# The last pair of experts: prompt sums first, sample rows by halves, one tile scaled by GpSimd

## What is computed

```python
hid = silu(einsum('becd,edf->becf', xs, w_gate)) * einsum('becd,edf->becf', xs, w_up)
out = einsum('becf,efd->becd', hid, w_down) * gate_vals[..., None]
moe = zeros_like(h).at[bidx, idx].add(out)
x = x + g2 * moe
y = rmsnorm(x, norm_final)          # y_prompt (128 rows), y_sample (512 rows)
```

## Time and profile before

| | us |
|---|---|
| median of three runs | 1007.59 |
| the three runs | 1007.21, 1007.59, 1008.83 |
| the profiled execution, its own time | 1008.96 |
| its span in the profile | 1007.2 |
| TensorE busy in the span | 965.1 (96%) |
| VectorE, ScalarE, GpSimd busy | 357.0, 294.7, 101.3 |
| mean granted TensorE clock | 0.990 of full speed |

### The profile page before, as it was taken

How to read it: one execution, slowest core, us unless ns; L and a number is a source line. 1 busy time by engine, 2 the same in 40 slices (tenths; PEclk the granted TensorE clock), 3 DMA queues, 4 the chain that set the end, 5 groups by cost and what they waited for, 6 DMA issues and landing times.

```text
span 1007.2 us, 18254 instructions
## 1 busy us (share of the span) xinstructions
PE 965.1 (96%) x7982; PEld 430.9 (43%) x7982; DVE 357.0 (35%) x806; ACT 294.7 (29%) x482; POOL 101.3 (10%) x112
## 2 busy tenths in 40 slices
PE   4999899999999899998999999999999999999996
PEld 3554456666666554463232332322323223232232
DVE  2476666463653563664021020210212102112115
ACT  5237756573653654323010010100101001010012
POOL 3200010000000011212001102011010110200100
PEclk9999999999999999999899999999999999999998
DMA  9990004504028441233999999999999999999982
GB/s 349 356 346 0 1 25 155 173 6 168 6 90 312 200 150 63 84 126 138 389 427 397 413 424 408 418 399 412 422 394 417 400 414 406 396 414 405 409 348 104
DMA packets 45218, 276.06 MB, mean 274 GB/s; under 512 B 3920, under 2 KB 4080, under 8 KB 32880
## 3 DMA queue, kind: packets, MB, share of 16 engines
q1 hardware_dynamic: 37824, 253.24, 62.2%
q0 software_dynamic: 5824, 16.81, 5.6%
q10 hardware_dynamic: 1520, 5.28, 1.4%
HBM read 262.30 MB, written 13.01 MB: 273 GB/s over the span
## 4 chain that ended last, share of the span: by engine, by line
PE 79%; DVE 7%; DMA 5%; ACT 3%; issue 3%; SPq 2%; POOL 1%; POOLq 0%; DVEq 0%
PE pa L538 52%; PE p L538 24%; DMA ring<-in_w_ada_dram 3%; DMA ring<-in_w_up_dram 1%; SPq L389 1%; ACT reg_c L1149 1%; PE pa L1043 1%; DMA reg_c<-h_rows,row_p 1%; ACT L1149 1%; PE p L981 1%; ACT reg_b L1149 1%; DVE reg_c L1550 1%; DVE reg_c L1595 1%; POOL reg_d L476 0%; ACT reg_d L1149 0%
## 5 line engine op out<-in xcount | busy, mean ns | idle before, releaser
L538 PE MATMUL pa<-ring,reg_b 128*32 128x512 f32 (+1 forms) x3232 | 412.8, 595 | 1.3 <-ACT reg_b L1149 1.2
L538 PEld LDWEIGHTS pa<-ring,reg_b 128*32 128x32 f32 (+1 forms) x3232 | 128.8, 114 | 256.3 <-issue 255.8
L538 PE MATMUL pa<-reg_a,ring 128*128 128x512 f32 (+1 forms) x768 | 229.6, 454 | 2.6 <-ACT reg_d L1149 2.6
L538 PE MATMUL p<-ring,reg_b 128*16 128x512 f32 x1536 | 172.9, 594 | 0.2 <-DMA ring<-in_w_up_dram 0.2
L538 PEld LDWEIGHTS pa<-reg_a,ring 128*128 128x128 f32 x768 | 119.3, 192 | 96.5 <-issue 96.4
L1149 ACT ACTIVATE reg_b<-pa 128x512 f32<-128x512 f32 (+1 forms) x36 | 21.1, 608 | 426.8 <-PE pa L538 262.1
L538 PEld LDWEIGHTS p<-ring,reg_b 128*16 128x16 f32 x1536 | 45.0, 97 | 121.3 <-issue 120.7
L1889 DVE TENSOR_TENSOR reg_b<-reg_b,p 128x512 f32<-128x512 f32 x8 | 5.5, 687 | 235.0 <-PE p L538 235.0
L1149 ACT ACT_TABLE_LOAD x64 | 82.1, 1283 | 4.2 <-issue 2.9
L1913 DVE SCALAR_TENSOR_TENSOR reg_c<-pa,slot_s,reg_c 128x512 f32<-128x512 f32 x14 | 10.5, 750 | 101.6 <-PE pa L538 101.6
L1149 ACT ACTIVATE reg_c<-reg_c 128x320 f32<-128x320 f32 (+1 forms) x86 | 43.3, 574 | 10.1 <-DVE reg_c L1601 9.2
(11 more groups left out here) (307 smaller groups left out, 742.9 us busy)
## 6 DMA issues: line engine op xcount, KB each, us to landing
ring<-in_w_gate_dram SPq DMA_DIRECT2D x32, 2048.0 KB, 14.5
ring<-in_w_up_dram SPq DMA_DIRECT2D x32, 2048.0 KB, 16.0
ring<-in_w_down_dram SPq DMA_DIRECT2D x32, 2048.0 KB, 17.7
ring<-in_w_ada_dram SPq DMA_DIRECT2D x12, 2048.0 KB, 8.0
ring<-in_w_in_dram SPq DMA_DIRECT2D x7, 2048.0 KB, 21.2
ring<-in_w_out_dram SPq DMA_DIRECT2D x2, 2048.0 KB, 19.2
sum_rows<-reg_a ACTq DMA_DIRECT2D x5, 512.0 KB, 2.7
h_rows<-reg_d POOLq DMA_DIRECT2D x5, 512.0 KB, 3.0
```

The lines of the kernel that those rows point to most:

```text
L538: return nc.tensor.matmul(out, lhsT, rhs, start=start, stop=stop, **kw)
```

## The change

In the last pair TensorE ends the prompt's down sums before the sample's second half begins, both halves of the prompt's in one go. It then does half of the first 512 columns of the sample's second sums, the prompt tile's two `add_rows`, the other half, and the last 512 columns. After that come all eight sample products in the order of `LAST_ROWS`: tiles 0 and 1 with their left halves, then with their right halves, then tiles 2 and 3. The PSUM tiles are given out anew in `last_in`. VectorE and ScalarE follow the new order: the prompt's tile is added, squared and scaled first, and the scalings of tiles 1, 2 and 3 come behind all additions. Tile 0 is no longer scaled by VectorE. GpSimd multiplies it by `nf_row` into `first_scaled` (the region `reg_b`), waits for the reciprocal from VectorE, multiplies again by that, and stores the tile from its own queue. SyncE stores the four other tiles, in the order 4, 1, 2, 3.

```diff
--- before.py
+++ after.py
@@ -213,6 +213,10 @@
         count_row = reg_e[:, 512:512 + T]
         g2q = reg_e[:, 0:512]
         which = reg_d[:, 2 * D:2 * D + T]
+
+        LAST_ROWS = [(4, 0), (4, 1), (0, 0), (1, 0), (0, 1), (1, 1), (2, 0), (2, 1), (3, 0), (3, 1)]
+        last_in = (p67, pa[0], p45, pa[1], pa[0])
+        first_scaled = reg_b[:, 0:D]
         out_q = reg_d[:, 2 * D + T:2 * D + T + 512]
         row_f = sp[:, 0:2, 0]
 
@@ -400,11 +404,11 @@
                     sp_eng.wait_ge(added[e][kind], 16 * (PAIRS - 1))
             for i in range(NT):
                 sp_eng.dma_start(acc[:, i, :], sum_rows[i * P:(i + 1) * P, :]).then_inc(back, 16)
-            for i in range(NT):
-                sp_eng.wait_ge(f_y, i + 1)
+            for n, i in enumerate((NT - 1, 1, 2, 3)):
+                sp_eng.wait_ge(f_y, n + 1)
                 dst = y_sample[0, i * P:(i + 1) * P, :] if i < NT - 1 else y_prompt[0]
                 sp_eng.dma_start(dst, acc[:, i, :]).then_inc(y_dma, 16)
-            sp_eng.wait_ge(y_dma, NT * 16)
+            sp_eng.wait_ge(y_dma, (NT - 1) * 16)
 
 
         @block.gpsimd
@@ -529,7 +533,15 @@
                 pool.sem_inc(out_free, 1)
             pool.wait_ge(g_s, 16 * PAIRS)
             pool.wait_ge(g_p, 16 * PAIRS)
-            pool.wait_ge(st_dma, 16 * (1 + 2 * HEADS))
+            pool.wait_ge(nf_in, 16)
+            pool.wait_ge(fin_add, LAST_ROWS.index((0, 1)) + 1)
+            nc.gpsimd.tensor_tensor(first_scaled, acc[:, 0, :], nf_row, ALU.mult).then_inc(pool_step, 1)
+            pool.wait_ge(pool_step, 4 + NT)
+            pool.wait_ge(h_ready, NT + 1)
+            nc.gpsimd.tensor_tensor(first_scaled, first_scaled, stat[:, 3, 0:1].to_broadcast([P, D]), ALU.mult).then_inc(pool_step, 1)
+            pool.wait_ge(pool_step, 5 + NT)
+            pool.dma_start(y_sample[0, 0:P, :], first_scaled).then_inc(st_dma, 16)
+            pool.wait_ge(st_dma, 16 * (2 + 2 * HEADS))
 
 
         @block.tensor
@@ -986,20 +998,19 @@
                     r = nc.tensor.transpose(dst[:, k * 32:(k + 1) * 32], xg_p[:, k * P:(k + 1) * P], ident[0:32, 0:32])
                 r.then_inc(xp_ps, 1)
 
-            def add_rows(i):
-
-                dst = (pa[0], p67, pa[1], p45, pa[0])[i]
-                if i == NT - 1:
-                    pe.wait_ge(fin_add, 2)
-                for half in range(2):
-                    cols = slice(512 * half, 512 * half + 512)
-                    pe.wait_ge(out_done, 3 * PAIRS + (1 + half if i < 3 else 3))
-                    if i < NT - 1:
-                        r = mm(dst[:, cols], which[:, i * P:(i + 1) * P], out_s[:, cols])
-                    else:
-                        rows = slice(64 * half, 64 * half + 64)
-                        r = mm(dst[:, cols], which[rows, TS:T], out_q[rows, :])
-                    r.then_inc(oh_ps, 1)
+            def add_rows(i, half):
+
+                cols = slice(512 * half, 512 * half + 512)
+                if i < NT - 1:
+                    pe.wait_ge(out_done, 3 * PAIRS + 2 + half)
+                    if i == 1:
+                        pe.wait_ge(fin_add, 2)
+                    r = mm(last_in[i][:, cols], which[:, i * P:(i + 1) * P], out_s[:, cols])
+                else:
+                    rows = slice(64 * half, 64 * half + 64)
+                    pe.wait_ge(out_done, 3 * PAIRS + 1)
+                    r = mm(last_in[i][:, cols], which[rows, TS:T], out_q[rows, :])
+                r.then_inc(oh_ps, 1)
 
             def pair(i, head, last=False):
                 def use(m, kh):
@@ -1114,16 +1125,17 @@
                     prompt_sums("d", 1, hidden_p, p45[:, 512:1024])
                 else:
 
+                    prompt_sums("d", 0, hidden_p, p45[:, 512:1024])
                     use("d", 1)
-                    sample_sums("d", 1, 0, hsT, pa[1]).then_inc(d_ps, 1)
+                    prompt_sums("d", 1, hidden_p, p45[:, 512:1024])
+                    sample_sums("d", 1, 0, hsT, pa[1], (0, 1))
+                    pe.wait_ge(which_done, 1)
+                    for t, half in LAST_ROWS[0:2]:
+                        add_rows(t, half)
+                    sample_sums("d", 1, 0, hsT, pa[1], (2, 3)).then_inc(d_ps, 1)
                     sample_sums("d", 1, 1, hsT, pa[1]).then_inc(d_ps, 1)
-                    prompt_sums("d", 0, hidden_p, p45[:, 512:1024])
-                    pe.wait_ge(which_done, 1)
-                    for t in range(3):
-                        add_rows(t)
-                    prompt_sums("d", 1, hidden_p, p45[:, 512:1024])
-                    for t in range(3, NT):
-                        add_rows(t)
+                    for t, half in LAST_ROWS[2:]:
+                        add_rows(t, half)
 
             pe.wait_ge(at_done, NT - 1)
             turn_rows(0)
@@ -1422,12 +1434,12 @@
                 rows_in(i + 1)
             hidden(PAIRS - 1)
             chain(A(stat[:, 2, 0:1], eps[:, 0:1], ACT.Sqrt))
-            for i in range(NT):
-                act.wait_ge(fin_add, 2 * i + 2)
-                if i >= 2:
-                    act.wait_ge(f_ss, i - 1)
-                A(h_tok[i % 2], acc[:, i, :], ACT.Square, accum_out=stat[:, 0, i:i + 1]).then_inc(f_ss, 1)
-                act.wait_ge(f_ss, i + 1)
+            for n, i in enumerate((NT - 1, 0, 1, 2, 3)):
+                act.wait_ge(fin_add, LAST_ROWS.index((i, 1)) + 1)
+                if n >= 2:
+                    act.wait_ge(f_ss, n - 1)
+                A(h_tok[n % 2], acc[:, i, :], ACT.Square, accum_out=stat[:, 0, i:i + 1]).then_inc(f_ss, 1)
+                act.wait_ge(f_ss, n + 1)
                 A(stat[:, 2, i:i + 1], stat[:, 0, i:i + 1], ACT.Sqrt, bias=eps[:, 0:1], scale=1.0 / D).then_inc(f_std, 1)
 
 
@@ -1948,41 +1960,37 @@
                 cols_ = slice(half * 512, half * 512 + 512)
                 V.tensor_tensor(out_s[:, cols_], pa[1][:, cols_], g2r[0][:, cols_], ALU.mult).then_inc(out_done, 1)
 
-            sample_out(0)
-            sample_out(1)
-
-            def add_rows(i):
-                src = (pa[0], p67, pa[1], p45, pa[0])[i]
-                if i == 0:
-                    dve.wait_ge(back, 16 * NT)
-                for half in range(2):
-                    cols_ = slice(512 * half, 512 * half + 512)
-                    dve.wait_ge(oh_ps, 2 * i + half + 1)
-                    V.tensor_tensor(acc[:, i, cols_], acc[:, i, cols_], src[:, cols_], ALU.add).then_inc(fin_add, 1)
-
-            def final_scale(i):
-                dve.wait_ge(f_std, i + 1)
+            def add_rows(i, half):
+                n = LAST_ROWS.index((i, half))
+                cols_ = slice(512 * half, 512 * half + 512)
+                dve.wait_ge(oh_ps, n + 1)
+                V.tensor_tensor(acc[:, i, cols_], acc[:, i, cols_], last_in[i][:, cols_], ALU.add).then_inc(fin_add, 1)
+
+            def final_scale(n, i):
+                dve.wait_ge(f_std, n + 1)
                 chain(V.reciprocal(stat[:, 3, i:i + 1], stat[:, 2, i:i + 1]))
                 V.scalar_tensor_tensor(acc[:, i, :], acc[:, i, :], stat[:, 3, i:i + 1], nf_row, ALU.mult,
                                        ALU.mult).then_inc(f_y, 1)
 
-            def prompt_out():
-                s, turn = chunk("d", 1, 1)
-                dve.wait_ge(freed[s], last * 2 + turn + 1)
-                V.tensor_tensor(out_q, p45[:, 512:1024], g2q, ALU.mult).then_inc(out_done, 1)
-
+            s, turn = chunk("d", 1, 1)
+            dve.wait_ge(freed[s], last * 2 + turn + 1)
+            V.tensor_tensor(out_q, p45[:, 512:1024], g2q, ALU.mult).then_inc(out_done, 1)
             dve.wait_ge(nf_in, 16)
-            add_rows(0)
-            add_rows(1)
-            final_scale(0)
-            add_rows(2)
-            final_scale(1)
-            prompt_out()
-            final_scale(2)
-            add_rows(3)
-            add_rows(4)
-            final_scale(3)
-            final_scale(4)
+            dve.wait_ge(back, 16 * NT)
+            add_rows(4, 0)
+            add_rows(4, 1)
+            sample_out(0)
+            final_scale(0, 4)
+            sample_out(1)
+            for i, half in LAST_ROWS[2:8]:
+                add_rows(i, half)
+
+            dve.wait_ge(f_std, 2)
+            V.reciprocal(stat[:, 3, 0:1], stat[:, 2, 0:1]).then_inc(h_ready, 1)
+            for i, half in LAST_ROWS[8:]:
+                add_rows(i, half)
+            for n, i in ((2, 1), (3, 2), (4, 3)):
+                final_scale(n, i)
 
 
 _INS = ["x_prompt", "x_sample", "state_lru", "state_hgrn", "c", "c_ctx", "w_ada", "b_ada", "norm_mix", "w_in",
```

## The result

The changed kernel is slower: 1011.46 us median of ten runs, against 1008.72 us for ten runs of the kernel before. The ratio is 1.0033 (95% interval 1.0025 to 1.0041); it is estimated from all the runs, and the quotient of the two medians alone is 1.0027. The forecast was 1008.2 us in a range of 1006.7 to 1009.5, and no difference that can be told, so it missed. Three single executions of the later measurements, two of the kernel before and one of the kernel with the last tile by halves, took 27% longer or more and are in no ratio.

The account below looks back on a forecast made before the run. TensorE was taken to carry the chain almost to the end, followed by VectorE's scalings and the stores. TensorE -1.01, scalings +0.56 and queued stores +1.10 gave +0.65 us on 1007.59, so 1008.2 us, range 1006.7 to 1009.5.

Parts of the forecast that it names:

- the sum: At the kernel's end: TensorE -1.01, three scalings in a row +0.56, queued stores +1.10, together +0.65 us.
- GpSimd's final wait for its store ends near 1004.5: End of GpSimd's queue: the wait for tile 0's store ends before SyncE's, with no cost in the sum.
- Without this cover: Earlier wait for `back`: loads land by about 978, addition needs them at 986.1, no cost; uncovered, the rest of that landing.
- the filled stall: TensorE's stall from 995.48 to 996.56, 1.08 us, is filled, so TensorE ends 1.01 us earlier, at 998.30.
- Three scalings at a pitch of 1.40 us: VectorE behind the last addition: scalings end at 1000.59, 1001.99 and 1003.39, where the last ended at 1003.84 before.
- The four stores: Last stores share the DMA engines, 5.20 us from 1001.42 to 1006.62, 0.65 us later than before; bounds 0.45 and 0.8.
- the product by the spread column: GpSimd's second product for tile 0, by the reciprocal: 997.73 to 1000.11, with its store issued at 1000.41.
- Exclusion between VectorE and GpSimd: First last scaling against GpSimd's second product: nothing or 0.9 us, equally open, said to hardly matter.
- The rival by which it costs 0.9 us: Stores free, VectorE held by GpSimd's product: last scaling ends at 1004.3, 0.45 us later than before, 1008.0 us; chance 0.14.
- a late second product: GpSimd's second product waits for all VectorE's scalings, its store ends 2.6 us later than before: 1010.2 us; chance 0.06.

Follow-up runs that it names:

- the last tile by halves: Against the kernel in which ScalarE, not GpSimd, makes tile 0's second scaling and stores it: tile 3 scaled and stored in two 512-column halves; ratio to before 1.0001.
- the product late: Against the changed kernel: VectorE makes tile 0's reciprocal behind all additions, so GpSimd's second product starts with VectorE's first scaling; one execution, 1013.52 us.
- before's order: Against the kernel before, in its own order: GpSimd makes tile 0's two products and stores it, SyncE stores the other four; ratio 0.9997.

## Why the prediction was wrong

**The step that failed** is the sentence ahead of the sum: "GpSimd's final wait for its store ends near 1004.5, before SyncE's." It was put at no cost. The wait did end before SyncE was through (1001.5 against 1005.2). But it is not the last thing on that queue. A drain of 7.8 us stands behind it, and the end of the program needs it. The row was in the trace of before, among the instructions of line 95. I had read the chain that ended last, which has no place for an instruction that is hidden, and I costed GpSimd's part only up to its last store. "Without this cover" was asked of the loads for `back`, but not of this. The stretch grew by 3.8 us, and the sum made without the drain said 0.65.

The drain alone would not have made the forecast exact. With the forecast's own 1004.5, a drain of 7.75 us and the 0.2 us from its end to the end of the span, the span ends near 1012.5, 5.3 us later than before. What came is 1.5 us less, because the wait ended 33.7 us after the start of the down sums and not 35.2: the second product was 0.5 us shorter, and the store landed 3.0 us after its issue, not 4.1 (1000.41 to 1004.5, for which the prediction shows no working). That landing was a second size put too high, and it went unnoticed because the whole wait was held to be free.

A part of the distance between 1008.2 and 1011.46 us is not the change at all. The forecast stood on a median of three runs, 1007.59 us, and ten runs gave 1008.72. With 0.65 us on top of that the time would have been 1009.4, inside the range.

**The other steps** held, in size too, but for one:
- TensorE was to gain 1.01 us from the filled stall. By the chains its sums ended 30.21 us after their start before (969.34 to 999.55) and 29.09 us after, a gain of 1.12 us. No gap turned up.
- Three scalings at a pitch of 1.40 us: they ended 1.38 and 1.39 us apart, and the last at the forecast point. ScalarE was in time for each.
- The four stores were to fill the engines for 5.2 us. They did, from 999.4 to 1004.7, and four times 512 KB in 5.2 us are 403 GB/s. Without the drain the end would have gone by them: SyncE's branch behind its last wait came 37.4 us after the start of the down sums (967.8 to 1005.2), 0.2 us more than the 37.2 of before (969.3 to 1006.5). The forecast had 0.65. The difference is a term that was oversized: the product by the spread column took 1.90 us, not 2.38, so GpSimd's store came 0.5 us earlier. The two rows of the changed kernel:

```profile
996.10 1.90 POOL L541 TENSOR_TENSOR reg_b<-reg_b,stat 128x1024 f32<-128x1024 f32 x1 [0.24 <-DVE stat L1989]
...
998.29 0.62 POOL L543 DMA_DIRECT2D out_dram<-reg_b  x1 [0.30 <-POOL reg_b L541]
```

- Exclusion between VectorE and GpSimd was rightly held to matter little. The first scaling of the changed kernel overlapped the product by only 0.3 us and took 1.37 us instead of 1.28. The rival by which it costs 0.9 us priced an overlap that the shorter product made impossible.
- The rival that lay on the side that came, a late second product, gave 1010.2 us (its own terms add up to 2.5 us and not 2.6, so to 1010.1), but by another mechanism. In the changed kernel the product started at 996.10, before any of the three last scalings. That its figure is the nearest to the measured one is chance.

Of the 3.8 us that the stretch grew, 0.2 us are SyncE's own way to the end, and the other 3.6 us are the time by which the drain outlasted it. Of these, 3.5 us came back when SyncE made the store and GpSimd's queue ended early, and 2.5 us when only the wait was moved.

## What to carry to other kernels

An engine that has long been idle at the end is not free to take a last job: look at what its queue still has behind its last wait, among the instructions of the program's end, and add that to the job's own end. On GpSimd that was 7.8 us here, so its last work has to end that long before the queue that waits for the last store is through, or it sets the end itself. A chain of waits shows what set the end of this kernel, never what is hidden and would set the next.

## What the runs showed of the hardware that was not expected

- GpSimd's closing drain takes 7.75 us where the queue had been idle for 50 us, 7.83 us behind a landed store, and ends 7.8 to 7.9 us after the end of a product or the issue of a store that was still running. It does not wait for the store's landing. What it does in that time, and whether a kernel without transfers from GpSimd's queue would have it shorter, was not tried and stays open.
- A GpSimd product of two full tensors of 128x1024 takes 2.37 to 2.38 us, and a product by one spread column 1.89 to 1.90 us with plain rows, where the permuted rows of line 476 took 2.38 us. Which of the two differences makes it faster there was not separated.
- A scaling that finds GpSimd's product running ends 1.08 us after the product's end (998.00 to 999.08 in the changed kernel, 1000.24 to 1001.32 with the product late, 992.09 to 993.17 in before's order), while alone it takes 1.28 us. So about 0.2 us of it pass during the wait.
